# Convolutions and Fourier mixing moved between the panels of the input projection, and a ninth expert panel in flight (float32, one core)

## The reference

```python
def mixer_sublayer(h, ...):
    p = h @ w_in
    q = qk_heads(p[..., OFF_Q:OFF_K], N_Q_HEADS, q_gain, rope)
    ...
    att = block_attention(q, concatenate([k, k_ext]), concatenate([v, v_ext]))
    hy = hyena_mixer(p[..., OFF_HY:OFF_FN], sw, sb, spec, hy_bias)
    fn = fourier_mix(p[..., OFF_FN:OFF_GATE])
    return merge_branches(att, hy, fn, p[..., OFF_GATE:], w_branch, w_out), k, v

def hyena_mixer(u, sw, sb, spec, bias):
    u = short_conv(u, sw, sb)            # three taps along the tokens
    v, g1, g2 = split(u, 3)
    z = g1 * long_conv(v, spec[:, 0], bias[0])   # by Fourier transforms of length 512
    return g2 * long_conv(z, spec[:, 1], bias[1])

def fourier_mix(u):                      # real part of a 2D transform: tokens, and 64 channels of a group
    ...

def expert_choice_moe(h, w_router, w_gate, w_up, w_down):   # 16 experts, 32 tokens each
    ...
    a, u = xg @ w_gate[e], xg @ w_up[e]
    y = (silu(a) * u) @ w_down[e]
    ...
```

## Time and profile before

| | |
|---|---|
| median of 3 runs | 2709.72 us (2707.25 to 2710.53) |
| the profiled execution | 2707.17 us, its span 2705.1 us |
| TensorE matmuls busy | 2285.5 us (84%) |
| VectorE, ScalarE busy | 822.3 us (30%), 394.8 us (15%) |
| DMA | 721.61 MB, mean 267 GB/s |
| mean granted TensorE clock | 0.925 of full speed |

### The profile page before, as it was taken

One profiled execution on the slowest core, in us unless ns is written; L12 is line 12 of the kernel. 1 busy time (PEld: TensorE's weight loads), 2 busy tenths in 40 slices (PEclk: granted clock), 3 DMA queues, 4 the chain that ended last, 5 costly groups with the idle time before them and its releaser, 6 DMA issues. The chain is left out here.

```text
span 2705.1 us, 29323 instructions
## 1 busy us (share of the span) xinstructions
PE 2285.5 (84%) x12064; PEld 1580.6 (58%) x12064; DVE 822.3 (30%) x1566; ACT 394.8 (15%) x862; POOL 6.1 (0%) x11
## 2 busy tenths in 40 slices
PE   8997977655656665656899999999999999999998
PEld 5785742111112111111788886788888888678887
DVE  5725631000001000000543267431034415753001
ACT  2203020000000000000200145210010004441000
POOL 0000000000000000000000000000000000000000
PEclk9999979788887778888999999999999999999999
DMA  9542679999999999999986321086358833106430
GB/s 382 220 169 109 270 328 427 426 428 427 428 428 427 429 428 427 429 426 426 389 300 235 126 91 63 11 358 255 140 217 301 306 131 117 63 1 238 151 125 16
DMA packets 74908, 721.61 MB, mean 267 GB/s; under 512 B 8625, under 2 KB 11697, under 8 KB 13233
## 3 DMA queue, kind: packets, MB, share of 16 engines
q1 hardware_dynamic: 74800, 720.09, 66.0%
HBM read 719.01 MB, written 1.05 MB: 266 GB/s over the span
## 5 line engine op out<-in xcount | busy, mean ns | idle before, releaser
L1601 PE MATMUL bank<-pool 128*128 128x256 f32 x2720 | 596.7, 381 | 6.2 <-ACT pool L1528 6.2
L1601 PEld LDWEIGHTS bank<-pool 128*128 128x128 f32 x2720 | 516.7, 191 | 82.1 <-issue 12.3
L1192 PE MATMUL bank<-pool,moe_x_cur 128*32 128x512 f32 x1792 | 259.3, 714 | 141.1 <-DMA pool<-in_w_expert 140.8
L1633 PE MATMUL bank<-trunk_proj,pool 128*128 128x256 f32 x1408 | 306.4, 379 | 0.0
L1633 PEld LDWEIGHTS bank<-trunk_proj,pool 128*128 128x128 f32 x1408 | 266.6, 190 | 36.6 <-issue 0.8
L1192 PEld LDWEIGHTS bank<-pool,moe_x_cur 128*32 128x32 f32 x1792 | 54.1, 120 | 329.7 <-DMA pool<-in_w_expert 224.5
L1208 PE MATMUL bank<-pool,moe_hidT 128*32 128x512 f32 x896 | 153.5, 822 | 76.5 <-DMA pool<-in_w_expert 68.6
L1820 PE MATMUL bank<-pool 128*128 128x256 f32 x672 | 148.1, 380 | 0.0
L1360 DVE TENSOR_TENSOR moe_hid<-bank,moe_silu 128x512 f32<-128x512 f32 x16 | 11.1, 692 | 446.6 <-ACT moe_silu L1316 446.6
L1820 PEld LDWEIGHTS bank<-pool 128*128 128x128 f32 x672 | 127.3, 190 | 19.9 <-issue 2.6
L1208 PEld LDWEIGHTS bank<-pool,moe_hidT 128*32 128x32 f32 x896 | 29.1, 132 | 181.0 <-DMA pool<-in_w_expert 113.0
(11 more groups left out here) (586 smaller groups left out, 2164.7 us busy)
## 6 DMA issues: line engine op xcount, KB each, us to landing
pool<-in_w_expert SPq DMA_DIRECT2D x168, 2048.0 KB, 35.6
pool<-in_w_ff SPq DMA_DIRECT2D x132, 1024.0 KB, 7.0
pool<-in_w_ada SPq DMA_DIRECT2D x66, 1024.0 KB, 7.0
moe_more<-in_w_expert SPq DMA_DIRECT2D x24, 2048.0 KB, 35.9
pool<-in_w_in SPq DMA_DIRECT2D x40, 1024.0 KB, 4.8
pool<-in_w_mod SPq DMA_DIRECT2D x24, 1024.0 KB, 7.8
pool<-in_w_out SPq DMA_DIRECT2D x10, 1024.0 KB, 9.9
pool<-in_small SPq DMA_DIRECT2D x2, 2560.0 KB, 13.2
```

What stands on the lines that cost most here:

```text
L1192: mm = pe.matmul(ps[b][quarter[g], :], x_cur[:, u], w[:, b, g], start=u == 0, stop=u == up_panels - 1)
L1601: mm = pe.matmul(self.ps[p % 3][:, j * T:(j + 1) * T], w[:, j * KD + k], self.hT[:, k], start=k == 0, stop=k == KD - 1)
L1633: mm = pe.matmul(self.ps[3 + q % 2][:, 0:T], w, x[:, k], start=k == 0, stop=k == nk - 1)
```

## The change

- The stage `hyena_fourier` is removed. Its `short_conv`, both `LongConv` and the Fourier mixing are done in `project_in`: on TensorE behind panels 8, 9, 11, 12, 13, 15 and 16, on VectorE between the w_mod panels 8 to 15, on ScalarE behind its takes 15 and 16. They work in `extra` and in the slot of the key and value panel, and in banks 6, 3 and 4 (halves of a bank share it).
- The last column sum is made behind panel 16 instead of 15, its transpose behind 17. `acc` uses its first half for tiles 0, 2 and 3, since the results of the mixing lie in the second; so w_mod panel 12 waits for the sum of tile 2.
- `attention` issues the `early` panels, has its scratch in another part of the ring, and has the value products in step 5 + 2p.
- In `moe` the first expert panel is loaded into `x_sel` at the stage's start; panel r is in slot (r - 1) % 8 from then on, and SP's waits count one panel more where slots are given to the feed-forward panels. VectorE waits for the end of the first panel before it writes `x_sel`.

```diff
-                for s in range(steps + 3):
+                for s in range(steps + 4):
 ...
-                    if s >= 4 and s % 2 == 0:
-                        values((s - 4) // 2)
+                    if s >= 5 and s % 2:
+                        values((s - 5) // 2)
...
+        self.turn_bank = banks[0]
+        self.bank = lambda f: banks[1 + f % 2][:, f // 2 * T:(f // 2 + 1) * T]
+        self.back = lambda ch: banks[0][:, ch * T:(ch + 1) * T]
...
     def dve_gate(self, ve):
+        ve.wait_ge(self.inverse, 2 * self.n + 2)
         for ch in range(2):
-            ve.wait_ge(self.inverse, 2 * self.n + ch + 1)
...
-        sum_behind = {4: 0, 8: 1, 12: 2, 15: 3}
+        sum_behind = {4: 0, 8: 1, 12: 2, 16: 3}
+        acc_of = lambda tile: acc[:, (0, 1, 0, 0)[tile]]
...
+                def fourier_first():
+                    pe.wait_ge(conv_mixed, 2)
+                    for n, (ch, t) in enumerate((ch, t) for ch in range(2) for t in range(NT)):
+                        mm = pe.matmul(ps[3 + ch][:, t * T:(t + 1) * T], x_fourier[:, ch, t * P:(t + 1) * P],
+                                       branch["fn_channel"], start=True, stop=True)
+                        if t == NT - 1:
+                            mm.then_inc(first_made, 1)
+
+                def fourier_second():
+                    pe.wait_ge(mid_out, 2)
+                    for ch in range(2):
+                        for n, (t, part) in enumerate((t, part) for t in range(NT) for part in range(2)):
+                            mm = pe.matmul(ps[3][:, ch * T:(ch + 1) * T], mid[:, ch, t, part * P:(part + 1) * P],
+                                           branch["fn_token"][:, t, part * T:(part + 1) * T], start=n == 0, stop=n == 3)
+                    mm.then_inc(second, 1)
...
+                    if p == 8:
+                        pe.wait_ge(short, 2)
+                        pe.wait_ge(other_out, 1)
+                        conv[0].pe_turn(pe)
+                    if p == 9:
+                        pe.wait_ge(by_sin, 3)
+                        conv[0].pe_transform(pe)
+                    if p == 11:
+                        conv[0].pe_inverse(pe)
+                    if p == 12:
+                        pe.wait_ge(conv_gated, 4)
+                        conv[1].pe_turn(pe)
+                    if p == 13:
+                        conv[1].pe_transform(pe)
+                    if p == 15:
+                        conv[1].pe_inverse(pe)
+                        fourier_first()
+                    if p == 16:
+                        fourier_second()
...
+                    if p == 15:
+                        for ch in range(2):
+                            sc.wait_ge(first_made, ch + 1)
+                            sc.activation(mid[:, ch], ps[3 + ch].rearrange("p (t n) -> p t n", t=NT), ACT.Copy)\
+                                .then_inc(mid_out, 1)
+                    if p == 16:
+                        sc.wait_ge(second, 1)
+                        sc.activation(fn_out, ps[3].rearrange("p (c n) -> p c n", c=2), ACT.Copy)
...
-                            ve.wait_ge(sums_made, tile - 1)
+                            ve.wait_ge(sums_made, (1, 3)[tile - 2])
...
                 for n in range(16):
+                    if n == 12:
+                        short_conv(2)
+                        ve.wait_ge(short, 4)
+                        conv[0].dve_gate(ve)
+                        conv[1].dve_copy(ve)
                     mod_panel(n)
...
+                    if n == 8:
+                        ve.wait_ge(signed, 1)
+                        ve.wait_ge(d.bank_free, 5)
+                        short_conv(0)
+                    if n == 10:
+                        ve.wait_ge(rotated, 3)
+                        conv[0].dve_copy(ve)
+                        short_conv(1)
+                    if n == 11:
+                        conv[0].dve_mix(ve)
+                    if n == 13:
+                        conv[1].dve_mix(ve)
                     if n % 4 == 3 and n > 4:
                         tile_add(n // 4 - 1)
+                ve.wait_ge(short, 6)
+                conv[1].dve_gate(ve)
                 tile_add(tiles - 1)
...
-                    sp.dma_start(expert_slots[u], I["w_expert"][0, u]).then_inc(expert_loaded[u], 16)
+                    sp.dma_start(expert_slots[u], I["w_expert"][0, u + 1]).then_inc(expert_loaded[u], 16)
...
+        lead_slot, lead_here = x_sel.rearrange("p k n -> p (k n)"), st.sem("lead_here")
...
                 sp.dma_start(numbers, cst["slots"]).then_inc(numbers_here, 16)
+                sp.dma_start(lead_slot, src[0, 0]).then_inc(lead_here, 16)
                 for u in range(6, slots):
-                    sp.dma_start(slot[u], src[0, u]).then_inc(slot_loaded[u], 16)
-                for r in range(slots, 2 * n):
+                    sp.dma_start(slot[u], src[0, u + 1]).then_inc(slot_loaded[u], 16)
+                for r in range(slots + 1, 2 * n):
                     sp.wait_ge(panel_done, r - slots + 1)
-                    sp.dma_start(slot[r % slots], src[r // n, r % n]).then_inc(slot_loaded[r % slots], 16)
+                    sp.dma_start(slot[(r - 1) % slots], src[r // n, r % n]).then_inc(slot_loaded[(r - 1) % slots], 16)
...
-                    sp.wait_ge(panel_done, E * n - slots + 1 + (u - 1) // 2 + 1)
+                    sp.wait_ge(panel_done, E * n - slots + 1 + (u - 1) // 2 + 2)
...
+                ve.wait_ge(panel_done, 1)
                 for half in range(2):
                     ve.wait_ge(x_first, half + 1)
```

More of the change, by code:

```diff
@@ L349, in __call__, with attention @@
         self.eng.wait_ge(self.sem, self.n)
-def attention(nc, c, ps, ar, q_of, k_of, v_of, out_of, n_pairs, n_keys):
+def attention(nc, c, ps, ar, q_of, k_of, v_of, out_of, n_pairs, n_keys, early):
     kt = n_keys // P
@@ L374, in attention, with _ @@
         with st.block() as block:
+            @block.sync
+            def _(sp):
+                for slot, src, sem in early:
+                    sp.dma_start(slot, src).then_inc(sem, 16)
             @block.tensor
@@ L463, in _ @@
                             turn_out(u)
-                    if s >= 4 and s % 2 == 0:
-                        store((s - 4) // 2)
+                    if s >= 5 and s % 2:
+                        store((s - 5) // 2)
 def sine(ve, link, out, x, tmp, quarter):
@@ L597, in project_in @@
         swapped, by_sin, by_cos, rotated = (st.sem("head_" + n) for n in ("swapped", "by_sin", "by_cos", "rotated"))
+        other_out, signed = st.sem("other_out"), st.sem("signed")
+        conv_sems = [st.sem("conv_" + n) for n in ("turned", "copied", "transformed", "products", "mixed", "inverse", "gated")]
+        conv_mixed, conv_gated = conv_sems[4], conv_sems[6]
+        centre, ahead, short, first_made, mid_out, second = (
+            st.sem(n) for n in ("centre", "ahead", "short", "first_made", "mid_out", "second"))
+        tall = lambda a, n: a.rearrange("p (k t) -> p k t", k=n)
+        kv_room = ring[:, KV_SLOT * BLK * P:(KV_SLOT + 1) * BLK * P]
+        u_conv, z_conv = tall(extra[:, 8 * T:14 * T], 6), tall(extra[:, 14 * T:16 * T], 2)
+        bufs = tall(extra[:, 4 * T:6 * T], NT), tall(kv_room[:, 0:4 * T], 4), tall(kv_room[:, 4 * T:8 * T], 4)
+        mid = kv_room[:, 4 * T:8 * T].rearrange("p (c t n) -> p c t n", c=2, t=NT)
+        v = lambda k, j=0, n=1: vec[:, V1[k][0] + j:V1[k][0] + j + n]
+        x_conv, x_fourier, hy_out, fn_out = proj[:, 4:10], proj[:, 10:12], spare[:, 4:6], spare[:, 6:8]
+        banks = ps[6], ps[3], ps[4]
+        conv = [LongConv(conv_sems, c, banks, bufs, branch, spec, 0, u_conv[:, 0:2], v("hy_bias", 0, 2), u_conv[:, 2:4], z_conv),
+                LongConv(conv_sems, c, banks, bufs, branch, spec, 1, z_conv, v("hy_bias", 2, 2), u_conv[:, 4:6], hy_out)]
         flat = lambda a: a.rearrange("p a b -> p (a b)")
@@ L1186, in _, with panel, up @@
             def _(pe):
-                def up(r, i, u):
-                    w = slot[r % slots].rearrange("p (b g n) -> p b g n", b=2, g=4)
-                    pe.wait_ge(slot_loaded[r % slots], i * (32 * n // slots) + (r // slots + 1) * 16)
+                def panel(r, i, first=False):
+                    if first:
+                        pe.wait_ge(lead_here, 16)
+                        return lead_slot
+                    at = (r - 1) % slots
+                    pe.wait_ge(slot_loaded[at], i * (32 * n // slots) + ((r - 1) // slots + 1) * 16)
+                    return slot[at]
+                def up(r, i, u, first=False):
+                    w = panel(r, i, first).rearrange("p (b g n) -> p b g n", b=2, g=4)
                     for b in range(2):
@@ L1203, in down @@
                 def down(r, i, s):
-                    w = slot[r % slots].rearrange("p (g b n) -> p g b n", g=4, b=2)
-                    pe.wait_ge(slot_loaded[r % slots], i * (32 * n // slots) + (r // slots + 1) * 16)
+                    w = panel(r, i).rearrange("p (g b n) -> p g b n", g=4, b=2)
```

(2 more changed lines are left out.)

148 lines of the change are left out of this document (43 added, 105 removed).

## The result

The changed kernel takes 2690.36 us, the median of four runs (2683.55 to 2691.87), the kernel before in the same comparison 2708.67 (2707.25 to 2710.53, four runs): a ratio of 0.9924, 95% interval 0.9912 to 0.9936, that is 17 to 24 us less; the ratio is estimated from all the runs and is not the quotient of the two medians, which lie 18.3 us apart. The forecast was 2693.3, from 2687.0 to 2699.5. The profiled execution of the changed kernel took 2691.83 (span 2690.0), 15.3 less than that of before.

What follows compares the result with a forecast made beforehand. TensorE bounds the projection, latency attention and the hyena stage, DMA the experts. -31.3 + 19.9 + 0.3 - 3.7 - 1.6 = -16.4 us takes 2707.17 to 2690.8, with the median 2.55 above it 2693.3; range 2687 to 2699.5.

Steps and rivals of the forecast that it cites:

- The stage goes away, -31.3: Hyena stage, from its first issue to the next stage's: all 31.3 us leave the path, boundary included.
- Its TensorE work between the panels, +19.9 and 0.3: Projection: the moved rows, transposes and joints add 19.9 us (19.0 to 21.5); clearing 15 more semaphores adds 0.3.
- VectorE's walk: Projection joints: VectorE's moved steps end before TensorE needs them, mixes near 157 and 195, smallest margin 3 us.
- Attention, -3.7: Attention: value products one step later no longer wait for ScalarE's copies, 3.7 us less, bounds 0 and 4.7.
- The ninth panel, -1.6: Expert stage: stream resumes 3.34 us later with one 4.91 us panel less to bring; gain 1.6, bounds 0 and 4.9.
- the trunk behind it moves with it as a block: Behind the experts: an earlier stream restart is gained one to one, the trunk moving along with the expert part's end.
- (a): Attention: keeps its length because another wait takes the place of the four; 2697 us, chance 0.12.
- (b): Project_out and expert head, 320 to 372 us: granted clock falls elsewhere, a fall spared or added; 2687 to 2697, chance 0.15.
- (c): Expert stream: ninth panel brings nothing, another transfer standing before it or restart later by a whole panel; 2695, chance 0.07.
- (d): Projection joints: VectorE is late, TensorE waits and its clock falls; 33 us at all nine, 2727, chance 0.05.

Runs made afterwards that it cites:

- the second: The changed kernel measured again, unaltered, against the kernel before: 2693.01 against 2709.94 us, ratio 0.9938 [0.9924, 0.9951].
- the delay of 12 us at one joint: The changed kernel with 26 chained VectorE operations in front of the first convolution's copy: 2702.65 us against 2708.64 before, ratio 0.9977.
- the one with the turns in front: The changed kernel with the value products in steps 4 + 2p, behind that step's turns: 2691.61 us, ratio 0.9937 to the kernel before.
- the second kernel with 3.7: The changed kernel with gathering products one panel later and unused products in the last expert: 2690.11 us, ratio 0.9926 to the kernel before.
- added products: The changed kernel with unused 128x512 products behind the last three up and first three down panels of the last expert: 2686.28 against 2708.64 us before.

## Why the prediction was right, and where it was not

The direction holds, the size lies in the range, and the mechanism holds for the move of the stage and for attention; that of the ninth panel failed at its last step. By its steps:

**The stage goes away, -31.3.** Its instructions and its boundary are gone; attention is followed by project_out at 257.73.

**Its TensorE work between the panels, +19.9 and 0.3.** Measured 170.40 - 150.46 = 19.94 us from the first product of the projection to the first score. ScalarE at the boundary, before and after, its last take and the first operation of attention:

```profile
206.50 0.60 ACT L729 ACTIVATE mixer_proj<-bank 128x512 f32<-128x512 f32 x1 [6.53 <-PE bank L707]
208.62 1.28 ACT L459 ACT_TABLE_LOAD   x1 [1.53 <-PEq L293]
```

```profile
225.78 0.60 ACT L790 ACTIVATE mixer_proj<-bank 128x512 f32<-128x512 f32 x1 [6.31 <-PE bank L749]
228.29 1.28 ACT L464 ACT_TABLE_LOAD   x1 [1.91 <-PEq L293]
```

By the measure of the prediction the boundary is 0.4 us longer (1.91 against 1.53), where I had 0.3 for the clears. TensorE's own idle grows by 0.16 only (2.37 against 2.21), because the pair of transposes that stood in front of the last panel now lies in the boundary, beside ScalarE's last take. That leaves 19.6 us for the rows and joints, and the pitches without that pair make 19.6: the joints cost nothing. VectorE's walk was right to 1.5 us at the first mix (done at 155.6 against 157) and to 3.5 at the second (191.5 against 195); both errors were on the safe side. VectorE in the changed kernel, the copy in front of the first transform and the last operation of the first mix:

```profile
143.85 0.69 DVE L528 COPY pool<-bank 128x512 f32<-128x512 f32 x1
...
154.90 0.68 DVE L541 TENSOR_TENSOR pool<-pool 128x512 f32<-128x512 f32 x1
```

**Attention, -3.7.** Measured 33.2 to 29.4, -3.8, in the two profiled executions, with a period of 6.05 us (forecast 6.1). What I didn't see is that the old order can cost more than the trace of before shows: in three of four traces the clock falls behind its 2.2 us wait, and 1.6 us are lost. The prediction noted that attention kept 1.00 through waits of 2.2 us; that held for that one execution and not for the next three. So the first pair of traces gives 3.8, and the medians 3.8, 4.5 and 7.7 us for the same lines. That all of the 7.7 comes from this fall isn't shown.

**The ninth panel, -1.6: this term was mis-sized.** It measured 0, by the runs (0.9999 [0.9990, 1.0008], which alone would still allow the 1.6) and more sharply by the start of the trunk in eleven traces. Three steps of the working hold: three transfers fit into the idle stretch, the restart is 3.34 us later, the stream has a panel less to bring. The last panel starts 1.1 us earlier against the first product in this trace (0.9 to 1.8 in all seven), near the 1.6. Then its own products take 3.4 us instead of 1.9, and 1.5 goes back. The step that failed is "the trunk behind it moves with it as a block": the last panel is the one panel of the stream whose duration on TensorE counts, and the earlier trace rows have the pair, 3.53 and 1.92 us, that shows that a panel may take either. I read them for the pitch alone. TensorE: Matmul & The Clock Gate of the Trainium skill, section "HAM oscillation — how this bites in real kernels", describes this pattern, bursts of matmuls of about 2 us with waits for transfers between them that start at half clock. The traces agree in part: 3.64 and 3.38 us behind waits of 1.27 us, and 1.92 with work in the gap. But by the Trainium skill every burst starts so, and in five traces without work in the gap the last panel took 1.92 us behind waits of 1.3 to 1.5.

**The sum.** -31.3 + 19.9 (clears included) - 3.8 - 1.1 + 1.5 = -14.8 at the trunk's start, against -16.4 forecast. The instants show -14.65; the rest are 0.3 us less in front of the projection and 0.4 more in project_out and the head of the expert stage, where nothing was changed but the third transfer. The medians give -18.3 in the first comparison and -16.9 in the second; the forecast's -16.4 lies just outside the first interval (17 to 24) and inside the second (13 to 21). The terms measured in the traces make -14.8, so the runs gained some 2 to 3.5 us more than the terms, where the forecast had 1.6 too much in the ninth panel. That the two errors nearly cancel in the time is luck. Single executions wander, which may be the reason: the trace of before happened to be one without the fall in attention (1.6 us) and cost 2707.17 where the median is near 2709. The trunk, which no edit here touches, took 1407.1 to 1407.7 us in eleven of the fourteen traces and 1401.7, 1404.1 and 1404.4 in three, so part of the scatter of the runs lies there. Whether these fill all of the difference isn't shown.

**The rivals.** (a) did not occur and was seen in another order, at 2.3 us. (b) occurs, but not as a shift by the change: the same kernel has the fall at the projection's start (1.7 us) or not, at attention's start (1.2 to 1.8) or not. The stretches that it named kept their lengths: project_out is 77.96 us against 77.79, the head of the expert stage 18.72 against 18.48. (c) came true in size, the ninth panel brings nothing, but for neither of its two reasons. (d) was priced by the delay of 12 us at one joint, which had 4.7 us of room; the narrowest had 3.1, the 3 of the walk.

**What stays open.** A restart 3.34 us later with a panel of 4.91 us less should give 1.57. Of it 0.45 is missing between the two profiled executions above, 0.2 to 0.6 in five of the seven traces and nothing in two (the kernel without the Fourier mixing and the one with the turns in front, where the last panel starts 910.0 and 910.1 us behind the first product); why isn't known. Why the last panel is slow each time with the restart at 5.3 us and fast with 2.0 or 3.7 is only told as a count, 7 of 7 against 4 of 4 and 1 of 1 (the second kernel with 3.7 had the added products too). The length of the last wait does not decide it: in the five fast cases without added products the panel before took 3.4 to 3.6 us and the wait was 1.3 to 1.5, while of the slow ones four came behind a panel of 1.92 and a wait of 3.0 to 3.4, and three behind one of 2.9 to 3.6 and a wait of 1.3 to 2.1.

## What to carry to other kernels

Independent work of a stage that is bound by latency cost only its pitch here when it was put between the panels of a stage that TensorE bounds, and the walk of the other engine's queue told beforehand that the joints hold. In a stretch that a stream of transfers bounds, look at how long the consumer's last item takes and at which clock: here it was the only one that counted, and it took back what the earlier end of the stream gave. A wait that was harmless in one trace may be followed by a fall of the clock in the next execution (2.2 us of wait and 1.6 of slow clock here), so removing such a wait in front of a burst can be worth more than its own length.

## What the runs showed of the hardware

A fall of TensorE's clock cost 1.7 us at the start of the projection, 1.2 to 1.8 at the start of attention, 1.6 behind a wait of 2.21 us in attention, 1.5 in the last expert panel, and 2.8 behind a wait of 7.62 us. A wait of 2.2 us was followed by a fall in three traces of four, with the same instructions in front of it. Bursts of 1.92 us of products (at the upper level) every 4.91 us left the clock going up and down (0.70 granted over 35 us), and 1.1 us more of products in each of the last gaps brought it to 0.89 and the last panels to 1.92 us, at no cost in time. Seven early panels, at 428 GB/s while they lasted, left the durations in attention as they were (the values' 16 products took 1.95 us beside them or not).
